# Where the second q chunk stands: before or behind the first stick-breaking scores

## What is computed

```python
for i in range(seqlen // SB_BLOCK):
    ...
    z = jnp.einsum("bhqd,bhkd->bhqk", qb, kp).astype(jnp.float32) * scale
    strict = jnp.arange(end)[None, :] < jnp.arange(start, end)[:, None]
    log_beta = jax.nn.log_sigmoid(z)
    log_keep = jnp.where(strict, jax.nn.log_sigmoid(-z), 0.0)
    suffix = lax.cumsum(log_keep, axis=3, reverse=True) - log_keep
    w = jnp.where(strict, jnp.exp(log_beta + suffix), 0.0)
    outs.append(jnp.einsum("bhqk,bhkd->bhqd", w.astype(vp.dtype), vp))
```

## Time and profile before

| | before |
|---|---|
| median of three runs | 1463.92 us |
| the profiled execution's own time | 1463.87 us |
| its span in the trace | 1462.1 us |
| what lies around the span | 1.77 us |
| PE busy | 1436.7 us (98%) |
| VectorE busy | 1164.0 us (80%) |
| ScalarE busy | 699.5 us (48%) |
| mean granted TensorE clock | 0.998 |

### The profile page before, as it was taken

The page is one execution under the profiler, slowest core; times in us unless marked ns, Lnnn a source line. Parts: engine busy times, 40 slices in busy tenths (PEclk is TensorE's granted clock), DMA queues, the critical chain, the costliest instruction groups (busy, mean ns, idle before and its releaser), DMA issues.

```text
span 1462.1 us, 23552 instructions
## 1 busy us (share of the span) xinstructions
PE 1436.7 (98%) x7907; PEld 1250.6 (86%) x7907; DVE 1164.0 (80%) x2216; ACT 699.5 (48%) x1238; POOL 317.6 (22%) x300
## 2 busy tenths in 40 slices
PE   8999989999999999999999999999999999999998
PEld 5877756599999999999999989888888888888887
DVE  6555572798999999899999955797878788888885
ACT  5454672233469733995459833443333333333331
POOL 1000200004023302231124532342222222322210
PEclk9999999999999999999999999999999999999999
DMA  7120304038679986799779999899999999999993
GB/s 303 44 73 0 145 14 160 1 116 301 197 253 357 402 294 222 275 397 378 246 254 376 417 410 386 328 366 353 334 338 349 339 330 362 332 380 348 354 345 145
DMA packets 175763, 403.02 MB, mean 276 GB/s; under 512 B 14672, under 2 KB 96592, under 8 KB 175184
## 3 DMA queue, kind: packets, MB, share of 16 engines
q1 hardware_dynamic: 138832, 268.02, 50.7%
q0 software_dynamic: 36864, 134.23, 25.1%
HBM read 347.67 MB, written 54.53 MB: 275 GB/s over the span
## 4 chain that ended last, share of the span: by engine, by line
PE 82%; DVE 8%; DMA 6%; ACT 2%; issue 2%; SPq 0%; POOL 0%; DVEq 0%; ACTq 0%
PE psum L536 46%; PE psum L1105 36%; DMA uraw<-in_uT 3%; DMA gates_scratch<-stage 1%; DVE ulo L1829 1%; DVE urow L1835 0%; DVE sco L1896 0%; DMA urow<-in_u,eidx 0%; ACT hotHi L1464 0%; DVE x L1707 0%; DVE sco L1932 0%; DVE sco L1948 0%; DVE routed L1940 0%; DVE itop L1894 0%; DVE itop L1900 0%
## 5 line engine op out<-in xcount | busy, mean ns | idle before, releaser
L536 PE MATMUL psum<-hhi,uhi 128*128 128x384 f32 x1024 | 348.3, 340 | 5.8 <-ACT act_s L1443 5.8
L536 PE MATMUL psum<-hlo,uhi 128*128 128x384 f32 x1024 | 342.6, 335 | 0.0
L1521 ACT ACTIVATE vhi<-vraw 128x1024 fp32r<-128x1024 f32 x128 | 135.8, 1061 | 329.3 <-PE psum L1105 326.5
L514 POOL DMA_INDIRECT urow<-in_u,eidx x128 | 159.0, 1242 | 532.9 <-DVE urow L1835 368.9
L1105 PE MATMUL psum<-vhi,whi 128*128 128x512 f32 x768 | 236.6, 389 | 0.0
L1105 PE MATMUL psum<-vhi,wlo 128*128 128x512 f32 x768 | 236.4, 389 | 0.0
L1105 PE MATMUL psum<-vlo,whi 128*128 128x512 f32 x768 | 236.4, 389 | 0.0
L2046 DVE TENSOR_TENSOR vlo<-vraw,vhi 128x1024 fp32r<-128x1024 f32 x128 | 156.7, 1224 | 75.9 <-ACT vhi L1521 75.0
L514 POOL DMA_INDIRECT urow<-in_v,eidx x120 | 134.9, 1124 | 369.5 <-DVE acc L2052 363.7
L536 PE MATMUL psum<-hhi,ulo 128*128 128x384 f32 x1024 | 198.8, 335 | 1.6 <-DVE ulo L1829 1.5
L536 PEld LDWEIGHTS psum<-hhi,uhi 128*128 128x128 f32 x1024 | 192.3, 188 | 7.4 <-ACT uhi L1436 6.9
(11 more groups left out here) (305 smaller groups left out, 1792.8 us busy)
## 6 DMA issues: line engine op xcount, KB each, us to landing
uraw<-in_uT SPq DMA_DIRECT2D x128, 512.0 KB
vraw<-in_v SPq DMA_DIRECT2D x128, 512.0 KB
acts_scratch<-act_s SPq DMA_DIRECT2D x128, 192.0 KB
gates_scratch<-stage SPq DMA_DIRECT2D x48, 512.0 KB
gring<-gates_scratch SPq DMA_DIRECT2D x32, 768.0 KB, 9.2
aring<-acts_scratch SPq DMA_DIRECT2D x128, 192.0 KB
wring<-in_chunks SPq DMA_DIRECT2D x18, 512.0 KB, 4.2
wout<-in_wout SPq DMA_DIRECT2D x1, 4096.0 KB, 12.7
```

The lines of the kernel that those rows point to most:

```text
L514: g.indirect_dma_start(urow[k], None, table, bass.IndirectOffsetOnAxis(eidx[:, n % HK:n % HK + 1], 0)).then_inc(row_in[k], 16)
L536: return nc.tensor.matmul(out, lhsT, rhs, start=start, stop=stop, skip_group_check=shared)
L1521: a_(vhi[:, k, :], vraw[:, k, :], ACT.Copy).then_inc(s["vhi_ready"], 1)
```

## The change

On PE, chunk `q1` is made ahead of `logits(0)` where it stood behind it. Behind that, each `kept` and `values(0)` with `logits(1)` come one chunk later: `k2` is made ahead of `kept(0)`, `z0` ahead of `kept(1)`, and `z1` ahead of `values(0)` and `logits(1)`. The list of jobs gets the same order, and so the banks are dealt out anew. Behind `z2` the order is the old one. The programs of the other engines don't change.

```diff
-PROJ = [("Z", 0), "q1", "k1", "q2", ("K", 0), "k2", ("K", 1), "z0", ("V", 0), ("Z", 1), "z1", "z2", "qm0", ("K", 2), "qm1",
+PROJ = ["q1", ("Z", 0), "k1", "q2", "k2", ("K", 0), "z0", ("K", 1), "z1", ("V", 0), ("Z", 1), "z2", "qm0", ("K", 2), "qm1",
         ("K", 3), "ssqm", "mk0", ("V", 1), ("Z", 2), "mk1", "rowm", "mv0", "mv1", ("K", 4), "mkss0", "mkss1", "qmss", ("K", 5)]
...
+            x_channels("q", 1)
             logits(0)
-            x_channels("q", 1)
             x_channels("k", 1)
             x_channels("q", 2)
+            x_channels("k", 2)
             kept(0)
-            x_channels("k", 2)
+            x_channels("z", 0)
             kept(1)
-            x_channels("z", 0)
+            x_channels("z", 1)
             values(0)
             logits(1)
-            x_channels("z", 1)
             x_channels("z", 2)
```

## The result

The changed kernel takes 1467.07 us, the median of ten executions (1464.68 to 1469.53), beside 1463.81 us for the kernel before (1461.54 to 1465.21): the ratio is 1.0027, with an interval from 1.0019 to 1.0035 (it is not the quotient of the two medians, which is 1.0022; the same holds for the ratios below). It is slower by 0.19 to 0.35%, above the 0.1% of the forecast. The profiled execution took 1467.12 us; its span is 1465.4 us, 3.3 us more than in the earlier trace rows, and PE is busy 3.4 us longer at the same work.

The account below looks back on a forecast made before the run. The prediction took PE's work and few gaps as the bound; - 0.94 us (gap gone) and + 2.36 us (new wait) summed to + 1.4 us, 1465.3 us, with an 8-in-10 range of 1463.6 to 1466.9 us.

Parts of the forecast that it names:

- The gap ahead of logits(0), - 0.94 us: PE's idle gap during VectorE's readout of `k0` would be covered by `q1`'s 24 matmuls, gaining 0.94 us.
- The stick-breaking chain moves as one, at no cost: From `logits(0)` through `logits(1)`, work would shift together by 4.50 us, with other engines' waits covered, costing nothing.
- The new wait, + 2.36 us start to start: PE would stand ahead of `z2` until VectorE reads `z1`, behind seven additions and one lowering of weights: 2.36 us.
- What is late next: Ahead of `kept(2)`, VectorE's `nklo` would finish with 2 us to spare, so no second wait.
- The rival in which the old fall at `kept(5)` goes: The clock's fall at 166.6 us would no longer happen, returning 1.7 us: 1463.6 us; chance 0.05.
- The sum, + 1.4 us: Whole kernel: - 0.94 + 2.36 = + 1.4 us, giving 1465.3 us; chance 0.70 for 1464.8 to 1465.9 us.
- The rival had said: The clock would fall once at PE's wait ahead of `z2`, losing another 1.7 us: 1467.0 us; chance 0.10.
- the argument against it: PE stood for 2.3 us before 864 us, with no matmul at all, and the clock stayed at 1.00.
- The range, up to 1466.9 us: Whole kernel's time, 8 in 10: 1463.6 to 1466.9 us, leaving out a clock fall at `z2` and the bare gain.
- the clock case: A clock fall during PE's wait ahead of `z2` would make the total + 3.1 us, 1467.0 us; chance 0.10.

Follow-up runs that it names:

- the three sets: The changed kernel timed three times against the kernel before: ratios 1.0027, 1.0027 and 1.0031.
- the wait filled: Changed kernel plus ten unread matmuls of 512 columns behind `logits(1)`, during PE's wait ahead of `z2`: 1463.64 us, ratio 1.0004 to the kernel before.
- third set: The changed kernel, unmodified, run again beside two kernels with added matmuls on the same chip: ratio 1.0031 to the kernel before.
- with seven matmuls more: Changed kernel plus seven unread matmuls of 512 columns between `k0` and `q1`: ratio 1.0025 to the kernel before.

## Why the prediction was wrong

- **The gap ahead of logits(0), - 0.94 us:** right. It is gone, and alone it gave - 0.8 us in the trace, twice.
- **The stick-breaking chain moves as one, at no cost:** right. `values(0)` was forecast near 110.2 us and came at 109.99 (`logits(0)` and `kept(0)` moved by 4.6 us, forecast 4.50); PE waited nowhere on the way.
- **The new wait, + 2.36 us start to start:** right. VectorE's own row says 112.41 for the copy and 117.89 for the readout of `z1`; PE restarts at 118.63, 6.22 us behind the copy's start, forecast 6.23. The bracket is 2.19 us, forecast "about 2.2". Taking the wait away took the loss away, and shrinking it to 1.05 us left + 0.5 us.
- **What is late next:** right, no second wait in the changed kernel. The rival in which the old fall at `kept(5)` goes didn't come either: it is there in all three profiles of the changed kernel.
- **The sum, + 1.4 us:** this step failed. It priced the wait by its length alone, with nothing for the clock behind it, and gave the fall a chance of 0.10. The fall came in all three profiles of the changed kernel, and made the chunk behind the wait 7.0 to 7.2 us long in place of 5.6 (a chunk behind a wait without a fall), 1.4 to 1.6 us. With it `kept(2)` is 3.0 to 3.2 us late behind `k0`, and 1.66 us late with the wait filled. The rival had said 1.7 us for the fall and 1467.0 us in all; that the median lies within 0.1 us of this is in part luck, since the medians of the three sets are 3.3, 4.8 and 3.8 us above those of before. The mean clock points the same way over many executions: 0.9966 in 25 of the changed kernel, 0.9980 in 87 of before. Were all of this PE's work, it would be 2.1 us in 1465, and + 3.5 us with the + 1.4 us of the gaps; this is an estimate on the high side, since the fall in the PEER part cost little. The three ratios are + 3.9 to + 4.5 us, each with over 1.1 us to both sides, so that they hold the 3.2 us of the trace and don't show whether more is lost.
- **Why it had so little chance:** the argument against it was one idle stretch of 2.3 us in one execution, behind which the clock stayed up. In the changed kernel's execution that very stretch had a fall behind it. One row of one execution showed that the clock may stay up, and I read it as showing that it does. By the count above, stretches of this length had a fall in 17 cases of 26. The Trainium skill, "TensorE: Matmul & The Clock Gate", section "A second HAM failure mode: psum-queue depth-cycling", tells of another kernel whose clock goes up and down because PE idles briefly and often between groups of matmuls. The traces here agree in so far as an idle stretch of 2.19 us had a fall behind it; it came once, between dense chunks, and no run here shows the case of frequent short ones.
- **The range, up to 1466.9 us,** left the clock case out by choice, by 0.1 us, and the measured 1467.07 us lies in that case. The three executions known to the forecast lay within 0.6 us; ten of before spread over 3.7 us, so that a single fall more or less is within the spread of single executions.

## What to carry to other kernels

Moving a unit of work on one engine moves it against the fixed order of the engine that reads its result: with a ring of buffers, look up which job's buffer the next one takes, and at which place of the reader's list that job is read. A new idle stretch of PE of 2 us isn't priced by its length alone: here it cost about 1.5 us more in five profiles of six, and useless matmuls in it took that cost away. Before a row of one execution is used to exclude a fall of the clock, ask whether the same stretch, or others as long, show one in other executions.

## What the runs showed of the hardware that was not expected

- The granted clock fell to 0.50 behind idle stretches of 2.1 to 2.2 us between dense matmuls in five profiles of six, not behind one of 1.05 us, and during one of 7.2 us. Over the whole of the fourteen profiles it fell at 17 of 26 idle stretches of 2.0 to 2.7 us, and at none of 42 of 0.9 to 1.8 us.
- The fall can come behind the restart: in the five profiles it came from 0.3 us ahead of it (changed kernel, third set) to 1.4 us behind it (with seven matmuls more), with PE busy in between.
- A fall lasted 3.3 to 3.4 us where PE was busy again at once, and went on for 4.7 us of work behind the wait of 7.2 us.
- The mean clock differs between executions of one kernel, from 0.995 to 0.999 in ten executions of the changed kernel. In these ten the time follows it closely (the fastest, 1464.68 us, had the highest, the slowest, 1469.53 us, the lowest), but not in the next set: there 1463.90 us had 0.996 and 1467.83 us had 0.998.
- Two other sources of spread stand in the traces: `k0` begins between 62.3 and 64.5 us (PE's first matmul between 5.2 and 6.8), and the stretch from 830 to 905 us, with transfers of expert weights in its chain, took from 1.3 us less to 3.7 us more than in the profile of before, in kernels that don't differ there.
